# The recurrence of an RWKV-7 time mix, per pair of heads: products of decayed keys in one group, the output's half products in one group, six masks ahead of the late ones

## The reference

```python
def rwkv7_step(S, inp):
    r_t, dec_t, k_t, v_t, kk_t, a_t = inp
    sa = jnp.einsum('bhij,bhj->bhi', S, -kk_t)
    S = (S * dec_t[:, :, None, :]
         + sa[..., None] * (kk_t * a_t)[:, :, None, :]
         + v_t[..., None] * k_t[:, :, None, :])
    y = jnp.einsum('bhij,bhj->bhi', S, r_t)
    return S, y
```

## Time and profile before

| | |
|---|---|
| median of 3 runs | 2564.7 us (2563.91 to 2565.28) |
| the profiled execution's own time | 2569.46 us |
| its span | 2567.7 us |
| mean granted TensorE clock | 0.984 |
| PE, DVE, ACT, POOL busy | 96%, 45%, 37%, 40% of the span |
| the recurrence | from 988.7 to 1197.3 us of the span |

### The profile page before, as it was taken

One profiled execution on the slowest core, in us unless ns is written; L12 is line 12 of the kernel. 1 busy time (PEld: TensorE's weight loads), 2 busy tenths in 40 slices (PEclk: granted clock), 3 DMA queues, 4 the chain that ended last, 5 costly groups with the idle time before them and its releaser, 6 DMA issues.

```text
span 2567.7 us, 32307 instructions
## 1 busy us (share of the span) xinstructions
PE 2474.2 (96%) x12240; PEld 1947.4 (76%) x12240; DVE 1163.6 (45%) x1981; ACT 937.4 (37%) x1582; POOL 1019.3 (40%) x617
## 2 busy tenths in 40 slices
PE   7999999999989889999999999999999899999998
PEld 5776577888857668886887888888767787888887
DVE  5113754213143666743723364164399533562462
ACT  3544553222246453323433323123333533322222
POOL 4331445444532222212552544345424443445344
PEclk9999899999999999999999999999999999999999
DMA  3222002333411110002431333233222221233232
GB/s 122 66 66 87 17 26 90 99 95 95 137 57 54 54 50 14 2 1 86 122 107 42 91 96 113 77 98 99 82 66 88 87 89 58 90 98 115 83 97 67
DMA packets 55579, 197.89 MB, mean 77 GB/s; under 512 B 6550, under 2 KB 8726, under 8 KB 54682
## 3 DMA queue, kind: packets, MB, share of 16 engines
q1 hardware_dynamic: 54509, 192.65, 24.4%
q10 hardware_dynamic: 941, 3.50, 0.4%
HBM read 194.03 MB, written 2.10 MB: 76 GB/s over the span
## 4 chain that ended last, share of the span: by engine, by line
PE 46%; DVE 7%; ACT 1%; issue 0%; DVEq 0%; ACTq 0%
PE ps L370 11%; PE ps L371 11%; PE ps L372 11%; DVE ps L2998 5%; PE ps L445 3%; PE ps L447 3%; PE ps L446 3%; PE ps L2841 1%; PE ps L2864 1%; PE ps L3011 1%; DVE ps L3160 0%; PE ps L2610 0%; PE ps L2614 0%; PE ps L2851 0%; PE ps L2641 0%; PE ps L3055 0%
## 5 line engine op out<-in xcount | busy, mean ns | idle before, releaser
L469 POOL TENSOR_TENSOR w_lo<-raw,w_hi 128x1024 fp32r<-128x1024 f32 x342 | 819.1, 2404 | 1008.2 <-ACT w_hi L461 1007.9
L370 PE MATMUL ps<-ahead_hi,w_hi 128*128 128x512 f32 x1216 | 481.0, 396 | 2.0 <-issue 2.0
L372 PE MATMUL ps<-ahead_hi,w_lo 128*128 128x512 f32 x1216 | 473.3, 389 | 0.0
L371 PE MATMUL ps<-ahead_lo,w_hi 128*128 128x512 f32 x1216 | 473.1, 389 | 0.0
L461 ACT ACTIVATE w_hi<-raw 128x1024 fp32r<-128x1024 f32 x342 | 352.8, 1049 | 171.0 <-PE ps L447 91.1
L370 PEld LDWEIGHTS ps<-ahead_hi,w_hi 128*128 128x128 f32 x1216 | 228.3, 188 | 53.3 <-issue 6.4
L371 PEld LDWEIGHTS ps<-ahead_lo,w_hi 128*128 128x128 f32 x1216 | 228.3, 188 | 50.6 <-issue 4.1
L736 DVE TENSOR_TENSOR x_stream<-x_stream,ps 128x512 f32<-128x512 f32 x79 | 54.3, 687 | 467.9 <-PE ps L372 277.9
L372 PEld LDWEIGHTS ps<-ahead_hi,w_lo 128*128 128x128 f32 x1216 | 228.3, 188 | 47.8
L3132 ACT ACTIVATE ffn_s<-ps 128x512 f32<-128x512 f32 x44 | 26.3, 598 | 322.3 <-DVE ps L3160 322.3
L445 PE MATMUL ps<-ffn_a_hi,w_hi 128*128 128x512 f32 x342 | 133.5, 390 | 3.0 <-DVE ffn_a_lo L3165 2.9
(11 more groups left out here) (433 smaller groups left out, 4580.4 us busy)
## 6 DMA issues: line engine op xcount, KB each, us to landing
raw<-in_wall SPq DMA_DIRECT2D x346, 512.0 KB, 3.6
x_stream<-in_x SPq DMA_DIRECT2D x8, 256.0 KB, 7.3
cw<-in_cmp_w SPq DMA_DIRECT2D x1, 2048.0 KB, 8.2
out_y<-x_stream SPq DMA_DIRECT2D x16, 128.0 KB, 1.8
lora_a<-in_lora_a ACTq DMA_DIRECT2D x1, 1152.0 KB
dist<-in_consts SPq DMA_DIRECT2D x1, 1088.0 KB, 11.2
lora_b<-in_lora_b ACTq DMA_DIRECT2D x1, 1024.0 KB
mem<-in_mem SPq DMA_DIRECT2D x1, 1024.0 KB, 5.0
```

Source lines behind the costliest of these rows:

```text
L370: pe.matmul(out, hi, src.hi[:, t, 0:width], start=first, stop=False)
L371: pe.matmul(out, hi, src.lo[:, t, 0:width], start=False, stop=False)
L372: return pe.matmul(out, lo, src.hi[:, t, 0:width], start=False, stop=last)
L469: e.tensor_tensor(self.w.lo[:, s, :], self.raw[:, s, :], as_float(self.w.hi[:, s, :]), ALU.subtract).then_inc(lo_r.sem, 1)
```

## The change

`SOON` goes from 5 to 6. The transposes of the next pair are cut in two parts of two kinds, with `sa_tensor` of block 1 between them. All eight units' products stand behind `state_tensor` of block 1, where four stood before it and four behind it. The matmul of `Ss` becomes `carried_tensor`, right behind each `sa_tensor` or the transposes; the eight half products of the output become one group behind `g_tensor`. `SA` gets four buffers, so that the waits for `y_sums` count pairs. VectorE masks units 0 to 5 in one run, copies `SA` of block 2, masks units 6 and 7, and makes their `MR` behind block 3; ScalarE copies the output behind G's copies. `t32_tensor` waits for six units at its first part and for the rest at its second.

```diff
-    SOON = 5
+    SOON = 6
...
-            late.tile("SA", 2, P)
+            late.tile("SA", NB, P)
...
-    def tokens_tensor(self, pe, p):
+    def tokens_tensor(self, pe, p, first, last):
...
-        wait(pe, "masked", 16 * p + 16)
+        wait(pe, "masked", 16 * p + 2 * self.SOON)
...
         done(mm, "l32")
+        wait(pe, "masked", 16 * p + 16)
...
+    def carried_tensor(self, pe, p, i):
+        self.wait(pe, "state_scaled", 3 * p + i)
+        self.done(pe.matmul(self.k.ps[:, 2, self.chunk(i)], self.Ss[:, i % 2, :], self.RA[:, 0, p, self.chunk(i)], start=False,
+                            stop=False, skip_group_check=True), "carried")
+
-    def y_tensor(self, pe, p, i):
+    def y_tensor(self, pe, p):
         k, wait, done = self.k, self.wait, self.done
-        wait(pe, "sa_made", NB * p + i + 1)
-        if i:
-            wait(pe, "state_scaled", 3 * p + i)
-            pe.matmul(k.ps[:, 2, self.chunk(i)], self.Ss[:, i % 2, :], self.RA[:, 0, p, self.chunk(i)], start=False,
-                      stop=False, skip_group_check=True)
-        for hh in range(2):
-            o = self.half(hh)
-            mm = pe.matmul(k.ps[o, 2, self.chunk(i)], self.SA[:, i % 2, o], self.MR[:, p % 2, NB * hh + i, :], start=False,
-                           stop=True, skip_group_check=True)
+        wait(pe, "sa_made", NB * p + NB)
+        for q in self.ORDER:
+            i, o = q % NB, self.half(q // NB)
+            mm = pe.matmul(k.ps[o, 2, self.chunk(i)], self.SA[:, i, o], self.MR[:, p % 2, q, :], start=False, stop=True,
+                           skip_group_check=True)
         done(mm, "y_sums")
...
-        n = NB * p + i
-        if n >= 2:
-            wait(v, "y_sums", n - 1)
+        if 3 * p + i >= 3:
+            wait(v, "carried", 3 * p + i - 2)
         done(v.tensor_scalar(self.Ss[:, i % 2, :], self.S[:, :], sm[:, i:i + 1], None, ALU.mult), "state_scaled")
...
     def tensor(self, pe):
...
             self.state_tensor(pe, p, 0)
             if more:
-                self.tokens_tensor(pe, n)
-            self.y_tensor(pe, p, 0)
+                self.tokens_tensor(pe, n, 0, 2)
             self.sa_tensor(pe, p, 1)
             if more:
-                for q in range(4):
-                    self.products_tensor(pe, n, q)
+                self.tokens_tensor(pe, n, 2, 4)
+            self.carried_tensor(pe, p, 1)
             self.state_tensor(pe, p, 1)
             if more:
-                for q in range(4, 8):
+                for q in range(8):
                     self.products_tensor(pe, n, q)
             self.sa_tensor(pe, p, 2)
-            self.y_tensor(pe, p, 1)
+            self.carried_tensor(pe, p, 2)
             if more:
                 self.u32_tensor(pe, n, 0, self.SOON)
                 self.ak_v_tensor(pe, n, 0, self.SOON)
...
             self.sa_tensor(pe, p, 3)
+            self.carried_tensor(pe, p, 3)
             if more:
                 self.t32_tensor(pe, n)
-            self.y_tensor(pe, p, 2)
-            if more:
                 self.u64_tensor(pe, n)
                 self.spread_late(pe, n)
-            self.y_tensor(pe, p, 3)
-            if more:
                 self.t64_tensor(pe, n)
                 self.seed_kv(pe, n)
                 self.g_tensor(pe, n)
+            self.y_tensor(pe, p)
+            if more:
                 self.seed_sa(pe, n)
                 self.seed_y(pe, n)
...
     def vector(self, v):
...
             self.scaled_vector(v, p, 1)
             self.sa_vector(v, p, 1)
-            if more:
-                for q in range(4):
-                    self.products_vector(v, n, q)
             self.state_vector(v, p, 1)
             self.scaled_vector(v, p, 2)
             if more:
-                for q in range(4, 6):
+                for q in range(self.SOON):
                     self.products_vector(v, n, q)
             self.sa_vector(v, p, 2)
             if more:
-                for q in range(6, 8):
+                for q in range(self.SOON, 8):
                     self.products_vector(v, n, q)
-                for q in range(self.SOON, 8):
-                    self.queries_vector_mask(v, n, q)
             self.state_vector(v, p, 2)
             self.scaled_vector(v, p, 3)
             self.sa_vector(v, p, 3)
+            if more:
+                for q in range(self.SOON, 8):
+                    self.queries_vector_mask(v, n, q)
```

More of the change, by code:

```diff
@@ L1737, in __init__ @@
             "sa_seed", "kv_seed", "y_seed", "sa_sums", "sa_made", "state_sums", "state_made", "state_scaled", "state_kept",
-            "state_zeroed", "y_sums", "y_taken", "spread_loaded")}
+            "state_zeroed", "carried", "y_sums", "y_taken", "spread_loaded")}
         k.advance(48, "lora_loaded")
@@ L2099, in place @@
         done(g.tensor_copy(self.Tb[0:32, :, 0:32], straight[0:32, :, at].rearrange("p t u -> p u t")), "placed")
-    def tokens_tensor(self, pe, p):
+    def tokens_tensor(self, pe, p, first, last):
         k, wait, done = self.k, self.wait, self.done
-        if p == 0:
+        if first:
+            pass
+        elif p == 0:
             wait(pe, "gathered", 4 * KD)
@@ L2115, in tokens_tensor @@
         wait(pe, "vec", 4 * KD)
-        for n, src in enumerate((self.RA[:, 1, p, :], self.rate[:, p, :], self.K[:, p, :], self.vv[:, p, :])):
+        for n in range(first, last):
+            src = (self.RA[:, 1, p, :], self.rate[:, p, :], self.K[:, p, :], self.vv[:, p, :])[n]
             for i in range(NB):
@@ L2161, in products_vector @@
         if p >= 2 and n == 0:
-            wait(v, "y_sums", 4 * (p - 1))
+            wait(v, "y_sums", p - 1)
         done(v.tensor_tensor(self.M[:, q, :, :].rearrange("p a t -> p (a t)"), bank[:, P:512], m4[:, P:512], ALU.mult), "masked")
@@ L2280, in state_tensor @@
         wait(pe, "sa_made", NB * p + i + 1)
-        done(pe.matmul(k.ps[:, 1, self.chunk(i)], self.BT[:, p % 2, i, :], self.SA[:, i % 2, :], start=False, stop=True,
+        done(pe.matmul(k.ps[:, 1, self.chunk(i)], self.BT[:, p % 2, i, :], self.SA[:, i, :], start=False, stop=True,
                        skip_group_check=True), "state_sums")
-    def y_tensor(self, pe, p, i):
-        k, wait, done = self.k, self.wait, self.done
-        wait(pe, "sa_made", NB * p + i + 1)
-        if i:
-            wait(pe, "state_scaled", 3 * p + i)
-            pe.matmul(k.ps[:, 2, self.chunk(i)], self.Ss[:, i % 2, :], self.RA[:, 0, p, self.chunk(i)], start=False,
-                      stop=False, skip_group_check=True)
-        for hh in range(2):
-            o = self.half(hh)
-            mm = pe.matmul(k.ps[o, 2, self.chunk(i)], self.SA[:, i % 2, o], self.MR[:, p % 2, NB * hh + i, :], start=False,
-                           stop=True, skip_group_check=True)
+    def carried_tensor(self, pe, p, i):
[3 more added lines that the diff above has]
+    def y_tensor(self, pe, p):
+        k, wait, done = self.k, self.wait, self.done
+        wait(pe, "sa_made", NB * p + NB)
[3 more added lines that the diff above has]
+                           skip_group_check=True)
         done(mm, "y_sums")
@@ L2336, in sa_vector @@
             wait(v, "sa_seed", p + 1)
[L2337 to L2340, removed]
+        if p:
+            wait(v, "y_sums", p)
+        done(v.tensor_copy(self.SA[:, i, :], k.ps[:, 0, self.chunk(i)]), "sa_made")
     def u32_scalar(self, act, p):
@@ L2395, in y_scalar @@
         k, wait, done = self.k, self.wait, self.done
-        wait(act, "y_sums", 4 * p + 4)
+        wait(act, "y_sums", p + 1)
         done(act.activation(self.RA[:, 0, p, :], k.ps[:, 2, :], ACT.Copy), "y_taken")
@@ L2417, in tensor @@
     def tensor(self, pe):
-        self.tokens_tensor(pe, 0)
+        self.tokens_tensor(pe, 0, 0, 4)
         for q in range(8):
@@ L2486, in scalar @@
                 self.u64_scalar(act, n)
-            self.y_scalar(act, p)
-            if more:
                 self.t64_scalar(act, n)
                 self.g_scalar(act, n)
+            self.y_scalar(act, p)
     def gpsimd(self, g):
```

## The result

The changed kernel takes 2569.62 us in the median of 19 runs, the kernel before 2565.83 in 19 runs: a ratio of 1.0018, 95% interval 1.0012 to 1.0024. It is slower by some 4 us, a little under the bound of 0.2% that the prediction had set, and outside its range of 2559.8 to 2567.3. Forecast was a gain of 2 us. (The forecast was added to a median of 2564.7 us in 3 runs; with 19 runs that median is 1.1 us higher, which doesn't bring the result into the range.)

A forecast was written before the change was run, and what follows sets the result against it. TensorE's own queue and waits were taken to bound the recurrence. Seven pairs at -0.35 (-2.45), +0.67 for the first pair and -0.3 for the last gave -2.1 us: 2562.6 from a median of 2564.7, range 2559.8 to 2567.3.

The forecast's parts named there:

- the bound of 0.2%: Whole kernel: a change under 0.2%, 5.1 us, can hardly be told from none.
- the term of the first pair: Ahead of the loop nothing covers the masks, so the first L2185 waits one unit more: +0.67 us.
- the rival of the clock: Loop: TensorE's clock falls because it stands 0.99 us a pair; 12.6 us slower, 2575.2 us; chance 0.04.
- The front, -0.32: Each pair before L2185: it waits for the sixth mask and starts at 8.50 instead of 8.82 us, gaining 0.32.
- the waits for banks: Front: units 5 to 7 wait for banks until units 0 to 2 are masked, hidden in TensorE's 0.99 us stand.
- The rival in which the masks don't bind: Front: all of TensorE's saving shows, 7 x -(1.31 + 0.03) = -9.4 us, total 2555.7 us; chance 0.11.
- The back, -0.03: Each pair from L2185 on: matmuls taken out and put in, with shape changes, sum to -0.03 us.
- The bound of 0.1 us for block 3: Back: block 3's sums need S of block 2, with 0.05 us left; taken as nothing, at most 0.1 a pair.
- GpSimd's copies: nothing, or 0.67: Front: Spc or Ss of block 2 loses nothing; rival, a copy goes first, +0.67 us a pair, 2567.3; chance 0.15.
- The loop: Seven pairs, each gaining 0.35 us from front and back together: -2.45 us.
- The last pair, -0.3: Last pair: half products leave block 1, eight follow the last SA; -0.3 us, ends -0.6 and +0.2.
- The expected 0.1 us at its start: Last pair: block 1's half products no longer stand between SA and the state product, about -0.1 us.

The follow-up runs named there:

- five ahead: The changed kernel with five instead of six units masked ahead in all pairs, late MR masks back in their old place: 2558.34 us, ratio 0.9969 to the kernel before.

## Why the prediction was wrong

The step that failed is the term of the first pair, +0.67 us: it priced the longer wait ahead of L2185 and took what TensorE's clock does behind it as nothing. The prediction did know the rival of the clock, but looked for a stand of TensorE in the loop alone, found the new one of the front, and gave it 0.04. What was missing is to ask of the first pair's wait what was asked of the loop's: what does TensorE do while it lasts, and what does its clock do behind it? The runs show 0.67 + 4.76 us there. Without the 4.76 the stretches of the two profiles would sum to -0.6 us, which lies inside the range.

Point by point, by the profiles:

- **First pair: +0.67.** Right as a wait (0.95 instead of 0.29 us), and short of the clock's 20.15 - 15.39 = 4.76 us. That the stand is the cause was shown by putting it in alone, taking it out alone, and filling it.
- **The front, -0.32.** Right: 8.47 us for 8.50, bounded by VectorE's six masks. That the waits for banks would be hidden was right as well, with less room than thought: TensorE arrives at 8.0 us, not at 7.51, because a unit let go alone takes 1.06 us and not 0.5. The two bounds of the front stood only half a microsecond apart, not 0.99, and with five ahead TensorE's own is the later one. The rival in which the masks don't bind would have given less than its 9.4 us.
- **The back, -0.03.** Measured 1162.52 - 1145.98 = 16.54, or +0.07. The bound of 0.1 us for block 3 was the right place: what is late there is `Ss`, not `S`.
- **GpSimd's copies: nothing, or 0.67.** Nearly nothing in six pairs (`Spc` of block 2 in 0.36 to 0.41 us instead of 0.29), and about 0.43 in pair 3. By the rule of the Trainium skill (SBUF — State Buffer, Who interferes with whom) whoever issues first of GpSimd and VectorE in its two-port mode holds the ports that they share for its whole instruction. The traces agree: `Spc` at 1141.17 us ends 0.08 us after the copy that was already running, and `Ss` at 1091.02 us ends 0.07 us after the copy that starts with it. Which of those two issued first, their recorded starts, 0.01 us apart, don't tell.
- **The loop.** 175.58 - 176.98 = -1.40 us, where -2.45 was forecast. Six pairs gained 0.24 to 0.30 each instead of 0.35, pair 3 lost 0.21.
- **The last pair, -0.3.** From its first state product to the next stage's first matmul 1197.25 - 1187.55 = 9.70 us instead of 9.58: +0.12. The expected 0.1 us at its start didn't come: the state product of block 1 follows the first by 2.05 us in both, at full clock, since it waits for VectorE's copy `SA` and not for the half products. From then on the clock decides. It averages 0.70 in that pair instead of 0.78, having fallen earlier. The sixteen half products take 1.98 us at the lower level, yet the output's copy starts 2.08 us after the last `SA` is made, against 2.13 before. Over all ten profiles this pair takes 8.20 to 10.09 us at mean clocks of 1.00 to 0.70, and 9.70 and 9.52 in the two of the unedited changed kernel. So neither the -0.3 nor the +0.12 can be told from one execution.
- **Sum by stretches.** 0.67 + 4.76 - 1.40 + 0.12 = +4.15 us; measured +3.8 by the medians. That these are so close is in part luck, as the last term shows.
- **That 0.2% can hardly be told.** The interval of 19 runs is 0.06% to each side, so a change of 0.18% could.

What stays open: why the second half of `S` is 0.17 us late in pair 3 of the new order, and how far the stand of pair 0 can grow before the clock falls. One of 0.66 us between the starts (0.29 named) did no harm and one of 1.33 (0.95 named) did; between them nothing was tried, and other work may shift the point.

## What to carry to other kernels

Where an edit makes TensorE wait longer, look at every place where it does, the first and last passes of a loop above all, and ask what the clock does behind each: here one wait that was 0.67 us longer cost more than seven pairs of a tighter loop brought in. If such a wait can't be avoided, try harmless work in it: ten transposes kept the clock up here. When two parts of a new order are tried, take each alone as well: one mask more ahead spoilt an order that with five ahead is 0.3% faster than the kernel before.

## What the hardware showed unexpectedly

In the changed kernel TensorE's clock fell to the lower level some 1.6 us after L2188 had begun, so during dense work and not in the wait. The windows of the changed kernel ahead of that point, behind it, and from the rise to the loop:

```profile
991.82:993.40 1.58, 1.58 (x14) 1.58 (x15) 1.18 (x4) 0.00 (x0) 0.00 (x0) 1.00 0.00 0
993.40:1003.60 10.20, 10.20 (x56) 9.86 (x56) 0.00 (x0) 1.72 (x4) 0.00 (x0) 0.50 0.00 0
1003.60:1011.97 8.37, 7.69 (x87) 6.20 (x86) 0.98 (x2) 3.07 (x8) 0.78 (x2) 1.00 0.01 2
```

L2199's twelve records take 2.32 us to the next start, where 1.34 is their time in the loop. Who looks for the cause where the clock is low looks in the wrong place. The fall came in three of three profiles of kernels with the longer stand, on at least two chips. Elsewhere slow stretches come and go between executions: the last pair has a mean clock of 0.70 in one profile and 1.00 in another. In the loop a stand of 0.47 us in each of seven pairs left the clock at 1.00.
